# Values behind the first scores, the output product's chunks reordered, and a down-projection's pass moved forward

## The reference, cut to what matters

```python
def attend(q, k, v):
    s = jnp.einsum('bqhd,bkhd->bhqk', q, k, preferred_element_type=jnp.float32) * ATTN_SCALE
    p = jax.nn.softmax(s, axis=-1).astype(v.dtype)
    return jnp.einsum('bhqk,bkhd->bqhd', p, v)
...
    q_l = mla_queries(cq_l, q_norm_w, w_uq, tabs)
    att_l = blocked_attend(q_l, k_all, v_all).reshape(b, l, MLA_OUT)
    conv_l = gb_l * short_conv(gc_l * xv_l, conv_w)
    out_l = jnp.concatenate([att_l, conv_l], axis=-1) @ w_out
...
def _conv_ffn(h, w_up, conv_w, w_down, rows, cols):
    u = _dwconv2d(h @ w_up, conv_w, rows, cols)
    a, b = jnp.split(u, 2, axis=-1)
    return (jax.nn.silu(a) * b) @ w_down
```

## Time and profile before

| | us |
|---|---|
| median of 3 runs | 2156.71 (2155.8 to 2156.82) |
| the profiled execution, its time | 2154.68 |
| the profiled execution, its span | 2152.9 |
| mean granted TensorE clock | 0.991 |

### The profile page before, as it was taken

One profiled execution on the slowest core, in us unless ns is written; L12 is line 12 of the kernel. 1 busy time (PEld: TensorE's weight loads), 2 busy tenths in 40 slices (PEclk: granted clock), 3 DMA queues, 4 the chain that ended last, 5 costly groups with the idle time before them and its releaser, 6 DMA issues.

```text
span 2152.9 us, 28628 instructions
## 1 busy us (share of the span) xinstructions
PE 2097.0 (97%) x11118; PEld 1752.4 (81%) x11118; DVE 1503.4 (70%) x2640; ACT 912.8 (42%) x1517; POOL 235.6 (11%) x149
## 2 busy tenths in 40 slices
PE   7999999999999999999999999989999999999998
PEld 5788888885788888888888888858888788879987
DVE  3777777766577776547467565768866487778995
ACT  4422222425452222225232233456555454656553
POOL 1000000006000000000000000031000000016861
PEclk9999999999999999999999999999999999999999
DMA  7555555341125555643555654525655333124544
GB/s 290 183 191 193 195 171 205 121 149 40 59 99 195 196 196 195 204 158 129 167 184 198 194 193 147 156 70 180 217 190 196 130 112 102 42 79 148 186 165 149
DMA packets 62390, 343.13 MB, mean 159 GB/s; under 512 B 6704, under 2 KB 8752, under 8 KB 32688
## 3 DMA queue, kind: packets, MB, share of 16 engines
q1 hardware_dynamic: 60528, 338.56, 45.7%
q10 hardware_dynamic: 1728, 2.75, 0.5%
HBM read 339.19 MB, written 1.05 MB: 158 GB/s over the span
## 4 chain that ended last, share of the span: by engine, by line
PE 85%; DVE 10%; ACT 2%; issue 1%; DMA 1%; POOL 0%; SPq 0%; DVEq 0%; ACTq 0%; POOLq 0%
PE bank L621 39%; PE bank L629 20%; PE bank L639 7%; DVE arena L2706 5%; PE bank L647 4%; PE bank L757 2%; PE bank L1036 1%; PE bank L766 1%; ACT w_hi L1302 1%; PE bank L669 1%; DVE w_lo L1897 1%; PE bank L1057 1%; PE bank L1138 1%; PE bank L1045 1%; DMA raw<-stream 1%
## 5 line engine op out<-in xcount | busy, mean ns | idle before, releaser
L1302 ACT ACTIVATE w_hi<-raw 128x1024 fp32r<-128x1024 f32 (+1 forms) x429 | 445.6, 1039 | 978.8 <-PE bank L621 875.4
L1897 DVE TENSOR_TENSOR w_lo<-raw,w_hi 128x1024 fp32r<-128x1024 f32 (+1 forms) x379 | 453.8, 1198 | 434.1 <-ACT w_hi L1302 429.1
L621 PE MATMUL bank<-h_hi,w_hi 128*128 128x512 f32 (+1 forms) x1288 | 428.8, 348 | 2.7 <-DVE h_lo L2392 1.3
L621 PE MATMUL bank<-h_lo,w_hi 128*128 128x512 f32 (+1 forms) x1288 | 426.3, 346 | 0.0
L621 PE MATMUL bank<-hidden_hi,w_hi 128*128 128x512 f32 x1024 | 398.4, 389 | 1.0 <-DVE squares L2129 1.0
L621 PE MATMUL bank<-hidden_lo,w_hi 128*128 128x512 f32 x1024 | 398.4, 389 | 0.0
L1930 DVE CUSTOM_DVE_ANT_0 scratch<-columns_raw,late,params 128x1024 f32<-128x1024 f32 x288 | 360.1, 1279 | 2.8 <-issue 2.4
L621 PEld LDWEIGHTS bank<-h_hi,w_hi 128*128 128x128 f32 x1288 | 243.8, 189 | 34.3 <-issue 2.3
L621 PEld LDWEIGHTS bank<-h_lo,w_hi 128*128 128x128 f32 x1288 | 243.9, 189 | 30.3 <-issue 0.5
L629 PE MATMUL bank<-h_hi,w_lo 128*128 128x512 f32 (+1 forms) x1288 | 266.2, 347 | 0.6 <-POOL w_lo L2815 0.3
L629 PE MATMUL bank<-hidden_hi,w_lo 128*128 128x512 f32 x1024 | 253.9, 389 | 0.0
(11 more groups left out here) (333 smaller groups left out, 2390.4 us busy)
## 6 DMA issues: line engine op xcount, KB each, us to landing
raw<-stream SPq DMA_DIRECT2D x221, 1024.0 KB, 5.0
columns_raw<-columns_in SPq DMA_DIRECT2D x176, 512.0 KB, 3.7
arena<-sides_in SPq DMA_DIRECT2D x6, 1024.0 KB, 10.2
x<-x_in SPq DMA_DIRECT2D x4, 512.0 KB, 16.0
late<-cond_in SPq DMA_DIRECT2D x2, 1024.0 KB, 4.9
columns_raw<-sides_in SPq DMA_DIRECT2D x1, 1024.0 KB, 22.8
late<-sides_in SPq DMA_DIRECT2D x1, 1024.0 KB, 24.1
arena<-arena ACTq DMA_DIRECT2D x2, 512.0 KB, 8.6
```

Source lines behind the costliest of these rows:

```text
L621: last = nc.tensor.matmul(acc, w_hi[:, buffer, kc, :], v(first_chunk + kc), start=start and kc == n == 0, stop=False)
L1302: nc.scalar.activation(w_hi[:, buffer, 0:chunks, :], raw[at % RING][:, 0:chunks, sub * P:(sub + 1) * P], ACT.Copy)\
L1897: nc.vector.tensor_tensor(w_lo[:, buffer, 0:chunks, :], raw[at % RING][:, 0:chunks, sub * P:(sub + 1) * P], w_hi[:, buffer, 0:chunks, :].b ...
```

## The change

Five things. (1) The four value steps leave `HEAD_STEPS`' loop and are issued behind the first three scores, into banks 0, 3, 6 and 7. Value 0 waits for all ropes (they read bank 0), value 1 for all query moves, value 2 for all key moves; behind value 3 PE waits for all value moves. ACT moves value 0 behind exponential 0, value 1 behind exponential 1, values 2 and 3 behind exponential 2. The first scores wait for three of the four key steps and the ropes of their own head only. (2) `rope(1)` is cut into three parts: heads 0 and 1 behind key 1, heads 2 to 4 behind key 2, heads 5 to 7 behind key 3. (3) ACT converts the first output half behind query 2, DVE at unit 4 of attention. (4) The first half of `out_product` takes chunks 4 to 7 first, waits for all but the last two `attended` at chunk 0 and for all at chunk 3. (5) In the last feed-forward block down's order begins (0,0), (0,1), (1,0), (0,2), (1,1), (1,2); the weight stream, the conversions, the updates and squares follow that list. A pass waits for its own group's hidden chunks only, and (1,0) for the taps of pair 20 as well. The same list is written for the other blocks with their old order.

```diff
+DOWN_STEPS = {name: [(pair, g) for pair in range(4) for g in range(len(GROUPS))] for name in ("10", "20", "11", "21")}
+DOWN_STEPS[""] = [(0, 0), (0, 1), (1, 0), (0, 2), (1, 1), (1, 2)] + [(pair, g) for pair in (2, 3) for g in range(len(GROUPS))]
+        VALUE_BANK = (0, 3, 6, 7)
+        ROPED_BEHIND = {1: (0, 1), 2: (2, 3, 4), 3: (5, 6, 7)}
 split_product, paired_product (PE)
-                for kc in range(chunks):
+                for m, kc in enumerate(order or range(chunks)):
+                    if order and kc in (0, KC // 2 - 1):
+                        pe.wait_ge(sem("attended"), awaited - (2 if kc == 0 else 0))
 down (PE)
-                    g, pair_of_chunks = j % len(GROUPS), j // len(GROUPS)
+                    pair_of_chunks, g = DOWN_STEPS[name][j]
                     full_wait(pe, at)
+                    if name == "" and (pair_of_chunks, g) == (1, 0):
+                        pe.wait_ge(sem("tap"), (UP - 1) * N_TAPS)
-                    pe.wait_ge(sem("hidden_ready"), hidden_before + min(KC * (g + 1), FC) if j < len(GROUPS) else hidden_before + FC)
+                    pe.wait_ge(sem("hidden_ready"), hidden_before + min(KC * (g + 1), FC))
 out_product (PE)
+                        order = None
+                        if attended_all and j == sub == 0:
+                            order = list(range(KC // 2, KC)) + list(range(KC // 2))
 mla_and_conv (PE)
+                def value(j):
+                    if j == 0:
+                        pe.wait_ge(sem("roped"), 11 * i + 3 + HEADS)
+                    elif j == 1:
+                        pe.wait_ge(sem(f"query_moved{tag}"), head_moves(len(HEAD_STEPS) - 4, t0 == 0))
+                    elif j == 2:
+                        pe.wait_ge(sem("key_moved"), 8 * i + HEADS)
...
-                pe.wait_ge(sem("roped"), 11 * i + 3 + HEADS)
                 pe.wait_ge(sem("key_rope"), 16 * (i + 1))
-                pe.wait_ge(sem("key_moved"), 8 * i + HEADS)
-                pe.wait_ge(sem(f"query_moved{tag}"), head_moves(len(HEAD_STEPS), t0 == 0))
+                pe.wait_ge(sem("key_moved"), 8 * i + 6)
...
+                        if n < 2:
+                            pe.wait_ge(sem(f"query_moved{tag}"), head_moves(4, t0 == 0))
+                            pe.wait_ge(sem("roped"), 11 * i + 3 + hd + 1)
...
+                    if n == 2:
+                        for j in range(4):
+                            value(j)
+                        pe.wait_ge(sem(f"query_moved{tag}"), head_moves(len(HEAD_STEPS), t0 == 0))
...
-                pe.wait_ge(sem("attended"), seen(i) // 2 + len(units) // 2)
                 pe.wait_ge(sem("conv_out"), 4 * i + 4)
-                out_product(f"out{i}", tag, t0, f"norm3{i}")
+                out_product(f"out{i}", tag, t0, f"norm3{i}", attended_all=seen(i) // 2 + len(units) // 2)
 mla_and_conv (ACT)
+                        if j == 2:
+                            convert(AT[f"out{i}", 0], 0)
-                convert(AT[f"out{i}", 0], 0)
...
+                    if n < 3:
+                        value_out(n)
+                    if n == 2:
+                        value_out(3)
 mla_and_conv (DVE)
-                        if j == 1:
-                            rope(1)
-                convert(AT[f"out{i}", 0], 0)
+                        if j in ROPED_BEHIND:
+                            rope(1, j)
...
+                    if n == 4:
+                        convert(AT[f"out{i}", 0], 0)
```

More of the change, by code:

```diff
@@ L612, in side_turn, with split_product @@
                 At.turned = b + 1
-            def split_product(acc, half, operand, chunks, first_chunk=0, begins_unit=False, start=True, stop=True):
+            def split_product(acc, half, operand, chunks, first_chunk=0, begins_unit=False, start=True, stop=True, order=None, awaited=None):
                 pe.wait_ge(half_high, half + 1)
@@ L632, in split_product, with paired_product @@
                 return last
-            def paired_product(acc, half, both, chunks, first_chunk=0, begins_unit=False, start=True, stop=True):
+            def paired_product(acc, half, both, chunks, first_chunk=0, begins_unit=False, start=True, stop=True, order=None, awaited=None):
                 pe.wait_ge(half_high, half + 1)
                 buffer = At.half % 2
-                for kc in range(chunks):
-                    last = nc.tensor.matmul(acc[:, :], w_hi[:, buffer, kc, :], both(first_chunk + kc), start=start and kc == 0,
+                for m, kc in enumerate(order or range(chunks)):
+                    if order and kc in (0, KC // 2 - 1):
+                        pe.wait_ge(sem("attended"), awaited - (2 if kc == 0 else 0))
+                    last = nc.tensor.matmul(acc[:, :], w_hi[:, buffer, kc, :], both(first_chunk + kc), start=start and m == 0,
                                             stop=False, skip_group_check=True)
-                    if kc == 0:
+                    if m == 0:
                         last.then_inc(half_begun, 1)
-                    if kc == 1 and begins_unit:
+                    if m == 1 and begins_unit:
                         last.then_inc(unit_begun, 1)
@@ L994, in mla_and_conv @@
                 pe.wait_ge(sem("latent_ready"), 3 * i + 3)
-                for n, (what, j) in enumerate(HEAD_STEPS):
+                def value(j):
[5 more added lines that the diff above has]
+                        pe.wait_ge(sem("key_moved"), 8 * i + HEADS)
+                    acc = bank[VALUE_BANK[j]]
+                    parts = 2 if j == 0 else 1
+                    for q in range(parts):
+                        some = slice(q * (T // parts), (q + 1) * (T // parts))
+                        last = nc.tensor.matmul(acc[:, some], latent[:, 2, j * P:(j + 1) * P], w_v[:, some], start=True, stop=True,
+                                                skip_group_check=True)
+                        if j == q == 0:
+                            last.then_inc(unit_begun, 1)
+                    last.then_inc(sem("head_sum"), 1)
+                for n, (what, j) in enumerate(HEAD_STEPS[:-4]):
                     acc = bank[IN_BANK[8 + n % 4]]
@@ L1004, in mla_and_conv @@
                             pe.wait_ge(sem("roped"), 11 * i + 2 + HEAD_STEPS[n - 4][1])
-                    if what == "value":
-                        parts = 2 if j == 0 else 1
-                        for q in range(parts):
-                            some = slice(q * (T // parts), (q + 1) * (T // parts))
-                            last = nc.tensor.matmul(acc[:, some], latent[:, 2, j * P:(j + 1) * P], w_v[:, some], start=True, stop=True,
-                                                    skip_group_check=True)
-                            if j == q == 0:
-                                last.then_inc(unit_begun, 1)
-                    elif what == "key":
+                    if what == "key":
                         last = nc.tensor.matmul(acc[:, :], w_k[:, j * P:(j + 1) * P], latent[:, 2, :], start=True, stop=True)
@@ L1602, in mla_and_conv, with value_out @@
                                                  scale=1.0 / width).then_inc(sem("latent_rms"), 1)
-                for n, (what, j) in enumerate(HEAD_STEPS):
+                def value_out(j):
+                    act.wait_ge(sem("head_sum"), 14 * i + len(HEAD_STEPS) - 3 + j)
+                    nc.scalar.activation(values[:, j, :], bank[VALUE_BANK[j]][:, :], ACT.Copy).then_inc(sem(f"query_moved{tag}"), 1)
+                for n, (what, j) in enumerate(HEAD_STEPS[:-4]):
                     if what == "key":
```

37 lines of the change are left out of this document (18 added, 19 removed).

## The result

The changed kernel took 2146.11 us (median of four executions, 2144.28 to 2147.3) against 2156.77 (2155.8 to 2157.19): a ratio of 0.9949, 95% interval 0.9938 to 0.9961. Two later comparisons of the same two kernels, on other chips, gave 0.9953 and 0.9951, gains of 9.9 and 9.5 us. The profiled execution took 2147.3 us, its span is 2145.5 us (before: 2154.68, 2152.9).

A forecast was written before the change was run, and what follows sets the result against it. PE was taken as the bound, busy for 97% of the span, so only its pauses could be regained: 1.1 + 1.65 + 2.65 + 2.2 = 7.6 us, giving a median of 2149.1 us, range 2146.6 to 2152.6 us.

The forecast's parts named there:

- The signs that the forecast names for being right: Transposes 6.4 and 8.7 us behind last query product; no pause before output products; (1,0) behind (0,1), POOL wait near 0.6 us.
- Layer 0: Attention of layer 0: with scores ahead of values, PE's transposes begin at 509.85 instead of 510.94, a gain of 1.1 us.
- Layer 1: Attention of layer 1: the same reordering brings the transposes from 1416.87 to 1415.2, a gain of 1.65 us.
- Chunks: Output products of both layers: chunks 4 to 7 first cover PE's 1.33 us pause in each, a gain of 2.65 us.
- down: Last block's turn from up to down: (1,0) ahead of (0,2) fills PE's wait for the last pair, gaining 2.2 us.
- The collision: Layer 0, DVE against POOL, chance 0.14: a 1.5 us pause goes (2147.6 us, 0.09) or DVE stretches (2150.6 to 2153.1, 0.05).
- the last of the sum: Whole kernel: the median lies 2.03 us above the profiled execution, so 2156.71 less 7.6 gives 2149.1 us.
- slower: Layer 1's value stretch: new pauses of 1.0 and 1.5 us lower the clock, gain gone or 2164 us; chance 0.02.
- The pause only moves: Attention, both layers: ACT's seven activations each take 0.2 us more, the 2.75 us gain is lost, 2151.9 us; chance 0.12.
- down's new pass is held up: Last block: ACT's list keeps PE as long as the pause that is removed, 2151.3 us; chance 0.05.
- a slower switch of the table: Layer 0: something behind ACT's table load holds it as long again, that part is lost, 2150.4 us; chance 0.05.

The follow-up runs named there:

- value_banks: The changed kernel with the values in banks 3, 6, 7 and 0 and ACT moving value 0 ahead of layer 1's exponentials: 2144.72 us, ratio 0.9943.
- the first set: Idle 128-column matmuls in PE's attention pauses: 5 and 13 in layer 0, 18, 5, 6 in layer 1 on the kernel before (2157.02 us); changed kernel with fillers, 2147.67 us.
- chunks alone: The kernel before with chunks 4 to 7 first in the first half of both output products, nothing else: 2153.43 us, ratio 0.9987.

## Why the prediction was wrong, point by point

- **The view of the kernel was right.** The signs that the forecast names for being right were seen, POOL's wait a little shorter; no single wait for ACT's value moves is over 2 us, and the clock stayed at 1.00 in attention. The gain is pauses of PE, at the named places, and it arrived at the end: behind each place the difference between the kernels' matmuls stays within 0.1 us until the next place or the next change of the clock.
- **Layer 0, 1.1 us forecast, 1.35 measured.** Chain, order and engine were as told. ACT's three exponentials and four moves took 3.43 us (506.68 to 510.11) where the sum had 3.6.
- **Layer 1, 1.65 forecast, 1.89 measured.** The same: 1.11 us of new pause ahead of value 0 (1.0 forecast), and 4.06 us of ACT's chain in place of 4.2.
- **Chunks, 2.65 forecast, 2.8 measured; down, 2.2 and 2.27.** Both right, POOL's wait 0.40 us where 0.6 was forecast.
- **The collision was a rival (0.09) and belonged in the sum.** It names its case, "this pause may go", and a shift of 1 us was certain. But the rows of a single instruction didn't say how the next ones would fall against POOL. It gave 0.68 us, a term that the sum had at nothing, and half of what the sum of 7.6 us lacks to the 9.0 us measured in the places; the rest is the three points above, 0.7 us together.
- **The failed step is the last of the sum:** the median "lies 2.03 us above that execution, so the median to expect is 2156.71 - 7.6". This carries the distance between the profile and the median over to the new kernel as if it were an overhead, and so puts what the change does to the clock at nothing. The profile of before was one of the executions without a fall of the clock in attention, and the median contained them. The change shortens the pauses behind which the clock falls, and in none of the eleven profiles with the new order did it fall there. That is worth about 1 us (0.9 by the mean clocks, 1.5 by the profiles).
- **The miss of 3.0 us in its parts:** 1.4 us are terms of the sum, the collision above all; about 1 is the clock's; the remaining 0.6 isn't explained, and is no more than the three comparisons differ among themselves (10.7, 9.9 and 9.5 us). Neither of the first two alone would have left the range.
- **Some luck is in how well the profile fits.** Against the profiled execution itself the places give 2154.68 - 9.0 = 2145.7 us, within 0.5 us of the median measured. But the profiles also differ where the change does nothing: by up to 1.5 us in what they bring from the start of the kernel, and by 1 us with the length of the fall near 1670 us. The profile of before was the earliest of the six at its start and had the longer of these falls.
- **The rival "slower" had the right mechanism and the wrong sign.** It asked whether the new pauses would bring the clock down, and took 1.00 between 1406 and 1417 us in one profile as evidence that the old ones did not. They did, in layer 1 in three of six profiles with the old attention. And a fall lasts some 3 to 7 us here and costs 1.1 to 1.7, where the rival reckoned with 15 us at the lower level and 7.6.
- **"The pause only moves", "down's new pass is held up", "a slower switch of the table"** did not happen. For the last: in the changed kernel the load ends at 506.67 and the next activation starts at 506.68. In value_banks, where the load is on the path, the move ahead of it ends at 1408.19 and the exponential starts at 1409.50: the switch costs 1.31 us in all. The Trainium skill, ScalarE: Activation LUTs, section What ACT_TABLE_LOAD costs, has 2.66 us; the trace disagrees, and the measurement decides.

What stays open: why the clock falls behind these pauses in one execution and not in the next, how much of the surplus is the clock's (0.9 or 1.5 us), and what is left of it, which the intervals don't resolve.

## What to carry to other kernels

Before adding a predicted gain to a median, ask why the median lies above the profiled execution: the others may have a loss that this profile happened to miss, and a change near its place can remove or bring it. Where TensorE's pauses sit close together, read several profiles for the granted clock; filling a pause with idle matmuls of the right length is a cheap test, and at the norms here a gain. When work is moved on an engine's queue, check what it is now ahead of: a table load that was hidden is 1.3 us as soon as something useful stands before it.

## What the runs showed that I had not expected

- A filler matmul of 128 fp32 columns leaves two records, which start 0.11 us apart at the upper level, so a filler takes 0.22 us; the first set was twice too long for that reason.
- A stall can cancel another: an execution that loses 2.2 to 3.1 us in layer 0 to the clock gets 1.1 to 1.5 us back, since its attention then meets POOL's two-operand instructions in another phase. The one that was 3.1 us late has no stretched difference of a head's output; those that were 2.2 us late have one, and two short pauses in place of the long one.
- In the first profile of the change the end of the kernel comes 0.37 us better than down's part explains. The last matmuls of the profile of before (`L823`) run behind a fall of the clock just ahead of the end; those of chunks alone do as well, with no gain there. The two later profiles of before show the same 0.36 us without any change. It is not of the change.
